# Two heads per key and query turn in the causal attention of a two-block transformer kernel, its first turn one round earlier, and three orders changed at seams

## The chip, the cores and the metric

The kernel runs on one core of one Trainium2 chip. The metric is the device time of one execution in microseconds (us); of the kernel before, three runs were timed, with a median of 1488.41 us (1486.58 to 1489.02). A core has TensorE (PE: matrix products and transposes into PSUM), VectorE (DVE), ScalarE (ACT), GpSimd (POOL) and SyncE (SP, which here only starts DMA transfers). Each engine works through its own list of instructions in order; semaphores tie them together.

## The reference, cut to what matters

Two blocks follow one another on x of 1024 tokens by 1024 channels: the first has grouped attention and a neighbourhood attention, the second a gated delta rule beside a dilated attention. All is float32. The change touches mainly the dilated attention of the second block:

```python
q, k, v = jnp.split(qkv, 3, axis=-1)                       # 8 heads of 64 channels
q = rms_norm(split_heads(q, ATT_HEADS), q_norm_w) * (ATT_HEAD_DIM ** -0.5)
k = rms_norm(split_heads(k, ATT_HEADS), k_norm_w)
for window, dilation in ((128, 1), (512, 4), (2048, 16)):
    o_p, lse_p = dilated_pattern(q, k, v, rel_bias, window, dilation)   # causal
o = sum(softmax(stack(lses)) * stack(outs))
```

The kernel computes the three patterns as one causal softmax over all keys, with a table that holds the bias and how many patterns a distance is in ("causal" below). Besides it, three small places are touched: the norm and projection at the start (`proj = rmsnorm(x) @ w_in`), the neighbourhood attention of block one ("near"), and the last rounds of the delta rule.

## The kernel before

**Products in float32.** Each product of float32 data is made from halves. A matrix is cast to a shortened form (`_hi`) by ACT, and DVE or POOL subtracts that from the original to get the rest (`_lo`). So every operand that is prepared costs a cast, then a subtraction that waits for it.

**Start (L405 to L450).** A token tile t of x is squared by ACT (L185), normalised by DVE (L194 to L201), turned by PE (L124, two halves of four 128x128 transposes), cast by ACT (L134) and subtracted by DVE (L140). PE then multiplies it by chunk 0 of the weights (L368). Chunk 1 of the weights comes through its own cast on ACT (L318, step t=3) and a subtraction on DVE (L334, `split_lo` at t=3). All later chunks are subtracted by POOL (`gpsimd`, L334).

**Near (L1195 to L1290).** Heads and row blocks are units u, two at a time. Every sixth unit ACT casts and DVE subtracts one 128-row piece kt of `w_out` (`ws.split_hi`, `ws.split_lo`), kt = u//6, from a transfer that SP started.

**Delta.** A chain of 16 chunks; the chunks of a round are inverted by a Newton-like iteration (L2158 and L2173 on PE, ACT copy L2452, DVE L2327 and L2330), whose result X is applied (L2184, L2196), and the state is stepped (L2215, L2230, L2239 on PE; L2349, L2358, L2369 on DVE). The order of every engine is written by hand with generators: `next(following)` lets the causal part put in its own steps between delta's, at eight places of the last two rounds, called round i=8 and round i=9 below.

**Causal (L2643 to L2960).** Eight heads with eight query blocks each make 64 units, ordered (7, 0, 6, 1, 5, 2, 4, 3) within a head. For a unit PE makes scores (L2785, L2786: query halves against one operand that holds the high key half on partitions 0 to 63 and the low one on 64 to 127), DVE adds the bias table and finds the maximum (L2865), ACT takes the exponential (L2927), PE transposes the probabilities (L2796), ACT or DVE copies them out (L2937, L2875), PE multiplies by v (L2810), and DVE divides (L2884). Before a head's scores, its keys and queries are turned in four parts ("preps": 512 tokens of k, 512 of k, 512 of q, 512 of q). For each part POOL writes the head's 64 channels twice side by side (`c_twice`, L2743), PE does four 128x128 transposes (L2773), ACT casts (L2922), DVE subtracts ("low", L2850 and L2852). Head h+1 is prepared in units 0, 1, 3 and 4 of head h, in PSUM bank 3. Head 0 is prepared in round i=9 of delta, each part in a PSUM bank of its own. After each unit's own work every engine does the unit's prep step, and none of it may be overtaken by what follows on the same engine.

```python
    PREP_AT = (0, 1, 3, 4)
    def prep_bank(h, part):
        return part + 1 if h == 0 else PREP_BANK
```

## Time and profile before

| | us |
|---|---|
| median of three timed runs | 1488.41 (1486.58 to 1489.02) |
| the profiled execution | 1485.48 |
| its span, as the profile has it | 1483.6 |
| PE busy | 1438.0 (97%) |
| DVE busy | 801.7 (54%) |
| ACT busy | 619.0 (42%) |
| POOL busy | 425.0 (29%) |

The clock granted to TensorE was full in all 40 slices of the profile (mean 0.997). A busy share says how much of the span an engine was at work; it does not say where PE, which is busy nearly all the time, still waits. That is read from the idle time that stands in brackets behind a row, with the instruction that ended it ("[1.37 <-DVE hT_lo L140]": 1.37 us idle, released by DVE's write of hT_lo at line 140). In a group of rows, "x8" means eight instructions in one stretch. The start of the span is time zero.

### The profile page before, as it was taken

Reading aid. Unit: us, or ns where it says so; the run is one execution under the profiler, and the core shown is the slowest. Engines: PE = TensorE matmul, PEld = TensorE weight load, DVE = VectorE, ACT = ScalarE, POOL = GpSimd, SP = SyncE. Lnnn points to the kernel's source line nnn. Section 1 sums busy time; section 2 is a strip of 40 time slices with the busy share of each in tenths; the row PEclk is TensorE's granted clock in tenths of the full one; section 3 lists DMA queues with packets and bytes.
Section 4 is the critical chain, followed back from the end, with each engine's and each line's share of the span. In section 5 each row is a group of like instructions: output and inputs, shape, how many; then the busy total and the mean of one; then the engine's idle time right before and its main releaser. Section 6 shows DMA issues by size and latency. Waiting matters only on the chain.

```text
span 1483.6 us, 30802 instructions
## 1 busy us (share of the span) xinstructions
PE 1438.0 (97%) x12682; PEld 1267.8 (85%) x12682; DVE 801.7 (54%) x1474; ACT 619.0 (42%) x1249; POOL 425.0 (29%) x527
## 2 busy tenths in 40 slices
PE   6999999989999999999999999999998998999998
PEld 6999998867777778878899999888897886888887
DVE  5238410149999878735420723452424776888431
ACT  5322121027777677632432113332325554777210
POOL 0212132110000277623202212221205884434320
PEclk9999999999999999999999999999999999999999
DMA  8313222000000043256325244433121021222342
GB/s 261 55 51 104 87 92 70 27 1 1 1 1 1 17 130 105 66 177 171 92 43 59 50 94 85 59 59 56 29 68 41 28 90 44 61 76 71 100 131 82
DMA packets 88017, 105.32 MB, mean 71 GB/s; under 512 B 25343, under 2 KB 72095, under 8 KB 87880
## 3 DMA queue, kind: packets, MB, share of 16 engines
q1 hardware_dynamic: 87880, 103.36, 27.0%
q8 instruction: 102, 1.67, 0.5%
q14 instruction: 35, 0.29, 0.1%
HBM read 80.20 MB, written 23.12 MB: 70 GB/s over the span
## 4 chain that ended last, share of the span: by engine, by line
PE 56%; DVE 4%; ACT 2%; DMA 1%; issue 1%; SPq 0%; POOL 0%; DVEq 0%; ACTq 0%
PE ps L368 22%; PE ps L1336 12%; PE ps L2810 2%; PE ps L1144 2%; PE ps L1128 2%; PE ps L2796 2%; PE ps L2785 1%; PE ps L2215 1%; PE ps L2158 1%; PE ps L2173 1%; DMA p_w_raw<-w_in 1%; PE ps L2773 1%; PE ps L1123 1%; PE ps L1122 1%; PE ps L2786 1%
## 5 line engine op out<-in xcount | busy, mean ns | idle before, releaser
L334 POOL TENSOR_TENSOR p_w_lo<-p_w_raw,p_w_hi 128x2048 fp32r<-128x2048 f32 (+1 forms) x27 | 127.3, 4716 | 506.9 <-ACT p_w_hi L318 506.9
L368 PE MATMUL ps<-p_w_hi,w_out_hi 128*128 128x256 f32 (+1 forms) x640 | 181.9, 284 | 0.4 <-ACT p_spill L393 0.3
L368 PE MATMUL ps<-p_w_hi,w_out_lo 128*128 128x256 f32 (+1 forms) x640 | 179.7, 281 | 0.0
L368 PE MATMUL ps<-p_w_lo,w_out_hi 128*128 128x256 f32 (+1 forms) x640 | 179.6, 281 | 0.0
L368 PE MATMUL ps<-p_w_hi,hT_hi 128*128 128x256 f32 x576 | 163.7, 284 | 1.9 <-DVE hT_lo L140 1.9
L368 PE MATMUL ps<-p_w_hi,hT_lo 128*128 128x256 f32 x576 | 162.7, 282 | 0.0
L368 PE MATMUL ps<-p_w_lo,hT_hi 128*128 128x256 f32 x576 | 162.6, 282 | 0.0
L368 PEld LDWEIGHTS ps<-p_w_hi,w_out_hi 128*128 128x128 f32 x640 | 120.5, 188 | 1.5 <-ACT p_spill L393 0.8
L368 PEld LDWEIGHTS ps<-p_w_lo,w_out_hi 128*128 128x128 f32 x640 | 120.8, 189 | 0.0
L368 PEld LDWEIGHTS ps<-p_w_hi,w_out_lo 128*128 128x128 f32 x640 | 120.6, 188 | 0.0
L368 PEld LDWEIGHTS ps<-p_w_hi,hT_hi 128*128 128x128 f32 x576 | 109.0, 189 | 2.3 <-DVE hT_lo L140 2.3
L318 ACT CAST p_w_hi<-p_w_raw 128x2048 fp32r<-128x2048 f32 (+1 forms) x28 | 53.5, 1909 | 137.0 <-DMA p_w_raw<-w_in 100.6
L368 PEld LDWEIGHTS ps<-p_w_lo,hT_hi 128*128 128x128 f32 x576 | 109.0, 189 | 0.0
L368 PEld LDWEIGHTS ps<-p_w_hi,hT_lo 128*128 128x128 f32 x576 | 109.0, 189 | 0.0
L897 ACT ACTIVATE tok<-ps,a_stat 128x1024 f32<-128x1024 f32 x64 | 72.4, 1131 | 43.6 <-DVE a_stat L848 43.6
L853 DVE TENSOR_TENSOR a_pt_lo<-ps,a_pt_hi 128x512 fp32r<-128x512 f32 x128 | 82.3, 685 | 15.3 <-ACT a_pt_hi L905 15.2
L393 ACT ACTIVATE p_spill<-ps 128x256 f32<-128x256 f32 x96 | 34.9, 385 | 132.9 <-PE ps L368 116.9
L905 ACT CAST a_pt_hi<-ps 128x512 fp32r<-128x512 f32 x128 | 68.8, 590 | 46.1 <-PE ps L794 46.1
L848 DVE TENSOR_REDUCE a_stat<-ps 128x1 f32<-128x1024 f32 x64 | 77.8, 1216 | 0.3 <-PE ps L784 0.3
L368 PE MATMUL ps<-w_out_hi,p_w_hi 128*128 128x512 f32 x192 | 76.2, 397 | 0.0
L368 PE MATMUL ps<-w_out_hi,p_w_lo 128*128 128x512 f32 x192 | 75.7, 394 | 0.0
L368 PE MATMUL ps<-w_out_lo,p_w_hi 128*128 128x512 f32 x192 | 75.5, 393 | 0.0
(299 smaller groups left out, 3585.0 us busy)
## 6 DMA issues: line engine op xcount, KB each, us to landing
p_w_raw<-w_in SPq DMA_DIRECT2D x26, 1024.0 KB, 8.0
s_gate<-p_spill SPq DMA_DIRECT2D x48, 128.0 KB, 1.8
kbT<-x SPq DMA_DIRECT2D x8, 512.0 KB, 6.9
b_w_raw<-w_out SPq DMA_DIRECT2D x8, 512.0 KB, 6.2
qT<-s_gate SPq DMA_DIRECT2D x8, 512.0 KB, 6.9
qT<-x SPq DMA_DIRECT2D x8, 512.0 KB, 3.5
s_x<-qT SPq DMA_DIRECT2D x8, 512.0 KB, 3.1
c_table<-s_line SPq DMA_DIRECT2D x8, 512.0 KB, 3.6
```

Source lines behind the costliest of these rows:

```text
L318: self.nc.scalar.copy(self.w_hi[:, c % 2, :, 0:w], self.raw[:, :, 0:w]).then_inc(self.w_hi_ready, 1)
L334: ops.tensor_tensor(self.w_lo[:, c % 2, :, 0:w], self.raw[:, :, 0:w], self.w_hi[:, c % 2, :, 0:w].bitcast(F32), ALU.subtract).then_inc(sel ...
L368: last = self.nc.tensor.matmul(out, lhs, rhs, start=(kt == 0 and i == 0), stop=(kt == KT - 1 and i == 2))
L393: op = self.nc.scalar.activation(dst, src, ACT.Silu if ch.silu else ACT.Copy)
L848: nc.vector.tensor_reduce(stat[:, 0, u:u + 1], s, AX.X, ALU.max, negate=True).then_inc(max_ready, 1)
L853: nc.vector.tensor_tensor(part(pt_lo, grp, half, i), ps[:, 4 + half, :].rearrange("p (c q) -> p c q", c=4), part(pt_hi, grp, half, i).bitc ...
L897: nc.scalar.activation(prob(u), s, ACT.Exp, bias=stat[:, 0, u:u + 1], accum_out=stat[:, 1, u:u + 1]).then_inc(prob_ready, 1)
L905: nc.scalar.copy(part(pt_hi, grp, half, i), ps[:, 4 + half, :].rearrange("p (c q) -> p c q", c=4)).then_inc(pt_hi_ready, 1)
L1128: last = nc.tensor.transpose(ps[:, 4 + u % 2, j * P:(j + 1) * P], prob[:, u % 4, j * P:(j + 1) * P], g.ident[:, :])
L1144: last = nc.tensor.matmul(ps[i * HD:(i + 1) * HD, 6 + u % 2, 0:HD], prob_t[:, u % 2, j * P + i * HD:j * P + (i + 1) * HD], value_tile(p, i ...
L1336: last = self.nc.tensor.matmul(self.ps[:, 4 + n % 4, :], a, b[:, kt, cols], start=(kt == 0 and i == 0), stop=(kt == KT - 1 and i == 2))
L2796: last = nc.tensor.transpose(ps[:, 4 + n % 2, (j - first) * P:(j - first + 1) * P], prob[:, u % 3, j * P:(j + 1) * P], g.ident[:, :])
```

## The change

Five things change.

1. **Preps by pairs of heads.** PE transposes 128 channels straight from the token tile `tok`, which are two heads at once. A set of four parts (now two of q, then two of k) serves a pair, so 16 transposes stand where 32 stood. The pair is prepared at units 2, 5, 8 and 11 of the sixteen units of the pair in front. POOL's copies `c_twice` go. ACT and DVE do two operations per part, one per head, on 64 partitions each. The second copy of a query half, on the other 64 partitions, is made by DMA from SBUF to SBUF (`double` on SP, four per q part), and scores wait for it (`q_doubled`). A key's low half goes to the other partitions by DVE's own write. There are four slots for keys and queries instead of two (`c_odd` is new).
2. **Pair 0 is prepared in round i=8** of delta instead of head 0 in round i=9, all four parts in one PSUM bank (bank 1). The scores of unit 0 go to banks 3 and 4, and stand before the last L2239 (`attend`).
3. **Start.** PE's first product waits for one half of tile 0 instead of both. The subtraction of weight chunk 1 moves from DVE to POOL.
4. **Near.** The cast and subtraction of `w_out` piece kt move six units later.
5. **SP** starts a head's bias table before its weight piece, instead of after.

The diff, cut to its core:

```diff
     def first_tensor(self, pe):
         self.norm.turn(pe, 0)
-        pe.wait_ge(self.norm.lo_ready, 2)
+        pe.wait_ge(self.norm.lo_ready, 1)
         self.multiply(pe, 0, 0, lambda: self.norm.turn(pe, 1))
...
             if t < NT:
                 self.norm.normalise(dve, t)
             self.norm.split_lo(dve, t - 1)
-            if t == 3:
-                self.split_lo(dve, self.nc.vector, 1)
...
-        pr.gpsimd(pool, 2, KEYS_AT + 1)
+        pr.gpsimd(pool, 1, KEYS_AT + 1)
...
-            if u % 6 == 4 and u // 6 < KT:
-                ws.split_lo(dve, nc.vector, u // 6)
+            if u % 6 == 4 and 0 < u // 6 <= KT:
+                ws.split_lo(dve, nc.vector, u // 6 - 1)
...
-            if u % 6 == 2 and u // 6 < KT:
-                ws.split_hi(act, nc.scalar.copy, u // 6)
+            if u % 6 == 2 and 0 < u // 6 <= KT:
+                ws.split_hi(act, nc.scalar.copy, u // 6 - 1)
...
-    k.sb("d_room2", [P, 2, H4, P])
+    g.osq = k.sb("d_osq", [P, 2, H4, P])[:, 0, :, :]
...
-    PREP_AT = (0, 1, 3, 4)
+    PREP_AT = (2, 5, 8, 11)
...
+        pair, at = u // (2 * NT) + 1, u % (2 * NT)
+        return [(pair, PREP_AT.index(at))] if at in PREP_AT and 2 * pair < ATT_HEADS else []
...
-        return 2 * (u % 2)
-        return part + 1 if h == 0 else PREP_BANK
+        return 2 * (u % 2) if u else 3
+        return 1 if pair == 0 else PREP_BANK
...
-    def half_of(t, h, part):
-        return t[:, h % 2, (part % 2) * 512:(part % 2) * 512 + 512]
+    def half_of(t, h, part, side):
+
+        return t[h % 4][side * HD:(side + 1) * HD, (part % 2) * 512:(part % 2) * 512 + 512]
...
+        def double(pair, part):
+            sp.wait_ge(low_ready, 8 * pair + 2 * part + 2)
+            for side in range(2):
+                h = 2 * pair + side
+                for m in (q_hi, q_lo):
+                    sp.dma_start(half_of(m, h, part, 1 - side).bitcast(F32), half_of(m, h, part, side).bitcast(F32)).then_inc(q_doubled, 16)
...
+        double(0, 0)
+        double(0, 1)
         sp.wait_ge(delta.s["o_summed"], NT)
         load_table(1)
         ws.load(sp, 0)
         ws.load(sp, 1)
         for h in range(2, ATT_HEADS):
+            if h % 2 == 0:
+                double(h // 2, 0)
+                double(h // 2, 1)
+            load_table(h)
             ws.load(sp, h)
-            load_table(h)
...
+        def turn_prep(pair, part):
+
+            if pair + part >= 1:
+                pe.wait_ge(low_ready, 8 * pair + 2 * part)
+            c0 = (0 if part < 2 else 512) + pair * P
             for j in range(4):
-                src = twice[:, part % 2, j, :, :].rearrange("p a d -> p (a d)")
-                last = nc.tensor.transpose(ps[:, prep_bank(h, part), j * P:(j + 1) * P], src, g.ident[:, :])
+                last = nc.tensor.transpose(ps[:, prep_bank(pair, part), j * P:(j + 1) * P],
+                                           g.att_tok[:, 4 * (part % 2) + j, c0:c0 + P], g.ident[:, :])
             last.then_inc(prep_turned, 1)
...
-            pe.wait_ge(low_ready, 4 * h + 4)
+            pe.wait_ge(low_ready, 8 * (h // 2) + 8)
+            pe.wait_ge(q_doubled, 128 * (h // 2) + 128)
...
-        for _ in range(4):
+        pe.wait_ge(delta.s["khatT_ready"], NT)
+        pe.wait_ge(delta.s["u_copied"], NT - 1)
+        for part in range(4):
+            turn_prep(0, part)
             yield
+        yield
+        yield
         pe.wait_ge(delta.s["attnT_ready"], NT)
         pe.wait_ge(delta.s["A_ready"], NT)
         pe.wait_ge(delta.s["X0_ready"], NT)
-        pe.wait_ge(delta.s["u_copied"], NT)
-        for part in range(4):
-            turn_prep(0, part)
-            yield
         scores(0)
+        yield
+        yield
         scores(1)
...
+        def low(pair, part):
+
+            bank = prep_bank(pair, part)
+            for side in range(2):
+                dve.wait_ge(high_ready, 8 * pair + 2 * part + side + 1)
+                turned_side = ps[side * HD:(side + 1) * HD, bank, :]
+                h = 2 * pair + side
+                if part < 2:
+                    hi, dst = half_of(q_hi, h, part, side), half_of(q_lo, h, part, side)
+                else:
+                    hi, dst = half_of(kk, h, part, side), half_of(kk, h, part, 1 - side)
+                nc.vector.tensor_tensor(dst, turned_side, hi.bitcast(F32), ALU.subtract).then_inc(low_ready, 1)
...
+        def high(pair, part):
+
+            act.wait_ge(prep_turned, 4 * pair + part + 1)
+            if pair >= 2:
+                act.wait_ge(scores_ready, NT * (2 * pair - 2))
+            for side in range(2):
+                dst = half_of(q_hi if part < 2 else kk, 2 * pair + side, part, side)
+                nc.scalar.copy(dst, ps[side * HD:(side + 1) * HD, prep_bank(pair, part), :]).then_inc(high_ready, 1)
```

In round i=8 of delta, PE's list shows where the four parts stand (L2773 was the prep's transpose; it is L2763 now, and all of delta's lines are two lower: L2158 is L2156, L2173 is L2171). Before, from the Newton step that follows the last L2196 but one:

```order
L2158 MATMUL ps<-d_X,d_Al 64x64 x8
L2173 MATMUL ps<-d_Z,d_T 64x64 x8
L2215 MATMUL ps<-d_S,d_wq 128x128 x4
L2158 MATMUL ps<-d_X,d_Al 64x64 x8
L2230 MATMUL ps<-d_vnew,d_ktail 64x128 x8
L2173 MATMUL ps<-d_Z,d_T 64x64 x8
L2158 MATMUL ps<-d_X,d_Al 64x64 x8
L2215 MATMUL ps<-d_S,d_wq 128x128 x4
L2173 MATMUL ps<-d_Z,d_T 64x64 x8
L2158 MATMUL ps<-d_X,d_Al 64x64 x8
L2230 MATMUL ps<-d_vnew,d_ktail 64x128 x8
L2173 MATMUL ps<-d_Z,d_T 64x64 x8
```

Now, with `tok` as the source of the preps:

```order
L2156 MATMUL ps<-d_X,d_Al 64x64 x8
L2171 MATMUL ps<-d_Z,d_T 64x64 x8
L2213 MATMUL ps<-d_S,d_wq 128x128 x4
L2763 MATMUL ps<-ident,tok 128x128 x4
L2156 MATMUL ps<-d_X,d_Al 64x64 x8
L2228 MATMUL ps<-d_vnew,d_ktail 64x128 x8
L2763 MATMUL ps<-ident,tok 128x128 x4
L2171 MATMUL ps<-d_Z,d_T 64x64 x8
L2156 MATMUL ps<-d_X,d_Al 64x64 x8
L2213 MATMUL ps<-d_S,d_wq 128x128 x4
L2763 MATMUL ps<-ident,tok 128x128 x4
L2171 MATMUL ps<-d_Z,d_T 64x64 x8
L2156 MATMUL ps<-d_X,d_Al 64x64 x8
L2228 MATMUL ps<-d_vnew,d_ktail 64x128 x8
L2763 MATMUL ps<-ident,tok 128x128 x4
L2171 MATMUL ps<-d_Z,d_T 64x64 x8
```

Each part from the second on stands directly in front of an L2171 group, or of one that leads to it. On DVE, in the same round, the subtractions of the preps (`c_q_lo`, `c_kk`) have come between; before:

```order
L2349 TENSOR_TENSOR d_vnew<-d_u,ps 64x512
L2358 TENSOR_TENSOR d_S<-d_Sg,ps 128x512
L2327 TENSOR_TENSOR d_X<-d_X,ps 128x256
L2330 STREAM_TRANSPOSE d_T<-d_X 128x256
L2349 TENSOR_TENSOR d_vnew<-d_u,ps 64x512
L2327 TENSOR_TENSOR d_X<-d_X,ps 128x256
L2330 STREAM_TRANSPOSE d_T<-d_X 128x256
L2358 TENSOR_TENSOR d_S<-d_Sg,ps 128x512
L2327 TENSOR_TENSOR d_X<-d_X,ps 128x256
```

Now:

```order
L2347 TENSOR_TENSOR d_vnew<-d_u,ps 64x512
L2850 TENSOR_TENSOR c_q_lo<-ps,c_q_hi 64x512 x2
L2356 TENSOR_TENSOR d_S<-d_Sg,ps 128x512
L2850 TENSOR_TENSOR c_q_lo<-ps,c_q_hi 64x512 x2
L2325 TENSOR_TENSOR d_X<-d_X,ps 128x256
L2328 STREAM_TRANSPOSE d_T<-d_X 128x256
L2347 TENSOR_TENSOR d_vnew<-d_u,ps 64x512
L2850 TENSOR_TENSOR c_kk<-ps,c_kk 64x512 x2
L2325 TENSOR_TENSOR d_X<-d_X,ps 128x256
L2328 STREAM_TRANSPOSE d_T<-d_X 128x256
L2356 TENSOR_TENSOR d_S<-d_Sg,ps 128x512
L2850 TENSOR_TENSOR c_kk<-ps,c_kk 64x512 x2
```

Two subtractions stand in front of each `d_S` or `d_X` that follows them. In the causal part, DVE's list in the third head (head 2) of before has two preps within five units, one subtraction each:

```order
L2865 ISA c_stat 128x1
L2875 COPY c_prob_t<-ps 128x512
L2850 TENSOR_TENSOR c_kk<-ps,c_kk 64x512
L2881 RECIPROCAL c_stat<-c_stat 128x1
L2884 TENSOR_SCALAR tok<-ps,c_stat 128x64
L2865 ISA c_prob,c_stat<-ps,c_table 128x256
L2865 ISA c_stat 128x1
L2850 TENSOR_TENSOR c_kk<-ps,c_kk 64x512
L2881 RECIPROCAL c_stat<-c_stat 128x1
L2884 TENSOR_SCALAR tok<-ps,c_stat 128x64
L2865 ISA c_prob,c_stat<-ps,c_table 128x768
```

At the same place now, two subtractions stand together behind the sixth unit's bias (768 wide) and its copy:

```order
L2862 ISA c_prob,c_stat<-ps,c_table 128x256
L2862 ISA c_stat 128x1
L2878 RECIPROCAL c_stat<-c_stat 128x1
L2881 TENSOR_SCALAR tok<-ps,c_stat 128x64
L2862 ISA c_prob,c_stat<-ps,c_table 128x768
L2862 ISA c_stat 128x1
L2872 COPY c_prob_t<-ps 128x384
L2850 TENSOR_TENSOR c_q_lo<-ps,c_q_hi 64x512 x2
L2878 RECIPROCAL c_stat<-c_stat 128x1
L2881 TENSOR_SCALAR tok<-ps,c_stat 128x64
L2862 ISA c_prob,c_stat<-ps,c_table 128x384
```

The order of the units' own work has not moved.

## Rows read from the trace of the kernel before

**Rows 1.** The page, part 1: engine, busy us, share of the span, instructions.

```profile
PE 1438.0 (97%) x12682; PEld 1267.8 (85%) x12682; DVE 801.7 (54%) x1474; ACT 619.0 (42%) x1249; POOL 425.0 (29%) x527
```

**Rows 2.** Windows: length, busy PE, PEld, DVE, ACT, POOL; sixth and last head, second without preps.

```profile
1334.16:1350.15 15.99, 15.81 (x222) 13.98 (x221) 14.06 (x42) 11.74 (x27) 5.77 (x6) 1.00 0.23 69
1366.12:1380.02 13.90, 13.77 (x209) 12.01 (x209) 12.07 (x40) 9.91 (x23) 4.11 (x4) 1.00 0.26 76
```

**Rows 3.** Groups by form, the preps' transposes: count, busy, mean ns, idle before.

```profile
L2773 PE MATMUL ps<-ident,c_twice 128*128 128x128 f32 x128 | 19.6, 275 | 3.0 <-DVE c_kk L2850 1.4 <-DVE c_q_lo L2852 1.3 <-DVE d_vnew L2349 0.3
```

**Rows 4.** Timeline of DVE (start, length): the first bias of heads 0, 1, 2.

```profile
1253.32 1.22 DVE L2865 CUSTOM_DVE_ANT_0 c_prob<-ps,c_table 128x1024 f32<-128x1024 f32 x1 [0.20 <-issue]
...
1269.23 1.22 DVE L2865 CUSTOM_DVE_ANT_0 c_prob<-ps,c_table 128x1024 f32<-128x1024 f32 x1
...
1286.18 1.22 DVE L2865 CUSTOM_DVE_ANT_0 c_prob<-ps,c_table 128x1024 f32<-128x1024 f32 x1 [0.16 <-PE ps L2786]
```

**Rows 5.** Timeline of ACT in head 0: the two table loads.

```profile
1264.71 1.28 ACT L3070 ACT_TABLE_LOAD   x1
...
1267.22 1.28 ACT L2927 ACT_TABLE_LOAD   x1
```

**Rows 6.** Waits of PE: engine and line waited for, total, times, longest.

```profile
PE ps L124 <- DVE hT_lo L140: 1.6, 2, 1.4
PE ps L2773 <- DVE c_kk L2850: 1.4, 2, 1.1
```

**Rows 7.** Timeline of the last rounds of delta, all engines.

```profile
1235.47 0.41 DVE L2327 TENSOR_TENSOR d_X<-d_X,ps 128x256 f32<-128x256 f32 x1
...
1238.52 0.42 DVE L2327 TENSOR_TENSOR d_X<-d_X,ps 128x256 f32<-128x256 f32 x1
...
1241.24 0.41 DVE L2327 TENSOR_TENSOR d_X<-d_X,ps 128x256 f32<-128x256 f32 x1
...
1241.71 1.09 PE L2184 MATMUL ps<-d_vb,d_X 64*64 64x128 f32 x16
...
1245.89 0.58 ACT L2922 CAST c_kk<-ps 128x512 fp32r<-128x512 f32 x1
...
1246.51 0.69 DVE L2850 TENSOR_TENSOR c_kk<-ps,c_kk 64x512 fp32r<-64x512 f32 x1 [0.54 <-ACT c_kk L2922]
...
1249.93 0.66 PE L2773 MATMUL ps<-ident,c_twice 128*128 128x128 f32 x4 [0.35 <-DVE d_vnew L2349]
...
1250.63 0.59 ACT L2922 CAST c_q_hi<-ps 128x512 fp32r<-128x512 f32 x1 [0.38 <-PE ps L2773]
```

**Rows 8.** Timeline of the start, ACT, DVE and PE.

```profile
20.07 1.91 ACT L318 CAST p_w_hi<-p_w_raw 128x2048 fp32r<-128x2048 f32 x1
...
22.02 2.29 DVE L334 TENSOR_TENSOR p_w_lo<-p_w_raw,p_w_hi 128x2048 fp32r<-128x2048 f32 x1
...
22.16 1.05 ACT L185 ACTIVATE qbT<-kbT 128x1024 f32<-128x1024 f32 x1
...
24.84 1.28 DVE L201 SCALAR_TENSOR_TENSOR qbT<-kbT,n_stat,qbT 128x1024 f32<-128x1024 f32 x1
...
26.04 1.28 DVE L140 TENSOR_TENSOR hT_lo<-ps,hT_hi 128x512 fp32r<-128x512 f32 x2
...
26.87 1.16 PE L124 MATMUL ps<-ident,qbT 128*128 128x128 f32 x8 [1.37 <-DVE hT_lo L140]
```

**Rows 9.** Timeline of DVE, the same three products at two places.

```profile
944.43 3.93 DVE L1912 SCALAR_TENSOR_TENSOR conv_y<-conv_in,p_conv_w,conv_y 128x1024 f32<-128x1024 f32 x3
...
994.13 8.18 DVE L1912 SCALAR_TENSOR_TENSOR conv_y<-conv_in,p_conv_w,conv_y 128x1024 f32<-128x1024 f32 x3
```

**Rows 10.** Timeline of POOL at the second of these places.

```profile
995.19 4.72 POOL L334 TENSOR_TENSOR p_w_lo<-p_w_raw,p_w_hi 128x2048 fp32r<-128x2048 f32 x1 [14.61 <-ACT p_w_hi L318]
```

**Rows 11.** Timeline of near, ACT and PE.

```profile
529.18 1.05 ACT L1287 CAST w_out_hi<-b_w_raw 128x1024 fp32r<-128x1024 f32 x1 [1.25 <-DMA b_w_raw<-w_out]
...
530.77 1.15 PE L1144 MATMUL ps<-b_v,b_prob_t 128*64 128x64 f32 x32 [0.95 <-ACT b_prob_t L1241]
```

More of the change, by code:

```diff
@@ L2653, in causal_part @@
     n_units = len(units)
-    PREP_AT = (0, 1, 3, 4)
+    PREP_AT = (2, 5, 8, 11)
     PREP_BANK = 3
-    v, table, kk, q_hi, q_lo = g.c_v, g.c_table, g.c_kk, g.c_q_hi, g.c_q_lo
-    prob, prob_t, twice = g.c_prob, g.c_prob_t, g.c_twice
+    v, table = g.c_v, g.c_table
+    kk, q_hi, q_lo = ([both[:, 0, :], both[:, 1, :], g.c_odd[:, n, 0, :], g.c_odd[:, n, 1, :]]
+                      for n, both in enumerate((g.c_kk, g.c_q_hi, g.c_q_lo)))
+    prob, prob_t = g.c_prob, g.c_prob_t
     ws = WeightSplit(nc, k, "c_w_", g.w_out2, w_hi, w_lo, g.c_raw, delta.weights)
@@ L2819, in tensor @@
         pe.wait_ge(delta.s["X0_ready"], NT)
-        pe.wait_ge(delta.s["u_copied"], NT)
-        for part in range(4):
-            turn_prep(0, part)
-            yield
         scores(0)
+        yield
+        yield
         scores(1)
@@ L2831, in tensor @@
             turn_probs(u)
-            for h, part in preps(u):
-                turn_prep(h, part)
+            for pair, part in preps(u):
+                turn_prep(pair, part)
             if u >= 2 and u % 2 == 0:
@@ L2885, in store @@
                                     None, ALU.mult).then_inc(out_stored, 1)
-        for _ in range(4):
-            yield
         for part in range(4):
             low(0, part)
+            yield
+        for _ in range(4):
             yield
@@ L2908, in vector @@
             empty(u)
-            for h, part in preps(u):
-                low(h, part)
+            for pair, part in preps(u):
+                low(pair, part)
         for u in range(n_units - 3, n_units):
@@ L2938, in empty @@
                                    ps[:, 4 + n % 2, 0:(end - first) * P]).then_inc(pt_by["act"], 1)
-        for _ in range(4):
-            yield
         for part in range(4):
             high(0, part)
+            yield
+        for _ in range(4):
             yield
@@ L2950, in scalar @@
             empty(u)
-            for h, part in preps(u):
-                high(h, part)
+            for pair, part in preps(u):
+                high(pair, part)
             if u + 2 < n_units:
```

53 lines of the change are left out of this document (6 added, 47 removed).

## The prediction

> **What bounds the kernel now.** I read the busy times first. PE is busy 1438.0 of 1483.6 us [rows 1], so the other engines count only where PE waits for them, and what is taken from PE counts only where nothing else comes last at once. The views after that were the windows by head, the groups by form, the waits of PE, and the timelines of the four places that the change touches. In the causal part a head takes, by the first window, 15.99 us with PE busy 15.81, DVE 14.06 and ACT 11.74 [rows 2]: PE sets the pace, and DVE has 1.93 us to spare. The last head, which prepares no follower, takes 13.90, by the second [rows 2]. So one set of 16 transposes is worth 15.99 - 13.90 = 2.09 us, or 131 ns each. The delta rounds are another regime: there PE waits at each step of a chain through PE, ACT and DVE. At the start PE waits for the low halves of the token tiles, 1.6 us in two waits [rows 6].
>
> **Causal part.** Before, seven heads (0 to 6) carry a set of 16 transposes for their follower. Now three pairs (0 to 2) carry one set each. Four sets go: 4 x 2.09 = 8.36 us, the most that can be had here. The reader should not multiply 64 removed transposes by their mean of 275 ns [rows 3]: that is 17.6 us, but the durations overlap, and the head's own windows say 131 ns. The Trainium skill, page "TensorE: Matmul & The Clock Gate", Part 4: PE-mode transpose, gives about 275 ns for one in a kernel's context. By that figure the four sets in the causal part would be worth 64 x 0.275 = 17.6 us; the row has the same 275 as a duration, and the windows show that it is no spacing.
>
> DVE decides what arrives of the 8.36. Its eight subtractions per pair and 14.06 us per head stay, while PE's period would fall to 15.99 - 1.05 = 14.94 per head, so DVE is at 94%. The two subtractions of a part stand together, 2 x 0.69 [rows 7], where a single 0.69 stood. The spare of DVE is (14.94 - 14.06) / 8 = 0.11 us per unit, so behind unit 5 about 0.5 of the second 0.69 reaches the bias of unit 8 and PE. I take 0.5 per pair, an estimate from these rows. Pairs 1 and 2 gain 2.09 - 0.5 = 1.59 each. Pair 0 has two table loads of 1.28 on ACT in front of a cast on which DVE waits in order [rows 5]; its two heads took 32.86 [rows 4] against 2 x 15.99 = 31.98 already. I put 0.24 more on it: 1.35. Head 6 had a set and has none now: 2.09. Sum: 2 x 1.59 + 1.35 + 2.09 = 6.6. Bounds: 8.36 if DVE's pairs of operations hide, 2.09 if DVE sets the period and only head 6 gains.
>
> The doubling DMAs are four of 64 x 512 floats per q part, 0.52 MB. The DMA moves 69 GB/s there at a share of 0.23 [rows 2], so some 300 GB/s in full: an estimate of 1.7 us per part, and 7.6 at the mean rate. The scores of the next pair come ten units (some 20 us) after the second q part, for pair 0 some 15 us. I cost them at nothing; with the cover gone it would be the 1.7 at pair 0. POOL's copies were off PE's path, and no gain. The table in front of the weights on SP is for a head later: nothing.
>
> **Seam.** Pair 0's four parts now stand in round i=8, where d_X follows at 1235.47, 1238.52 and 1241.24 and the apply at 1241.71 [rows 7]. All four share a PSUM bank. So a part costs, as a chain: from its transposes to the cast 1250.63 - 1249.93 = 0.70, from the cast to the subtraction 1246.51 - 1245.89 = 0.62, and two subtractions of about 0.67 with their spacing: 2.65 us. In that time the next part's transposes wait on PE, with delta's L2171 (L2173 before) behind them, and DVE stands at the subtraction with delta's d_X and d_S behind it. I laid delta's steps out around this. The first d_X has two parts in front of it, of which one overlaps other waits: 1235.47 becomes 1238.1. Part 2 lies between it and the next, and takes 5.0 instead of 3.05: 1238.52 becomes 1243.1. Part 3 comes before the third, 4.4 instead of 2.72: 1241.24 becomes 1247.5. The apply starts at about 1248.0 instead of 1241.71: +6.3. Round i=9 is freed of its four parts. Its own chain (S times wq, v_new, S) ran at its pace with them; only behind the last v_new they stood on it, at 1249.93 where PE did transposes before L2239. That and the scores in front of it give back 0.7. The first bias moves from 1253.32 [rows 4] to 1258.9: **+5.6**. Bounds: -0.7 (all four parts vanish in PE's waits of round 8) and +6.3 (nothing is given back). I take 5.6, since both queues are in order and the bank admits one part at a time. Before, each had its own bank and no part waited for a part.
>
> **Start.** DVE's subtraction of chunk 1 takes 2.29 at 22.02, in front of tile 4's chain: L201 at 24.84, hT_lo at 26.04, and PE's turn at 26.87 after 1.37 idle [rows 8], 2.03 behind the start of L201. Taken away, that chain starts when ACT's square L185 is done, 22.16 + 1.05 and a read-out, at 23.4. Two small operations between took 0.53 (from 24.31, the subtraction's end, to 24.84); L201 would begin at 23.95, and PE at 26.0: -0.9. Waiting for one low half of tile 0 lets PE begin up to 0.6 earlier, but chunk 1's transfer and cast, which come next, do not move; I cost that at nothing (at best -0.5, so -1.4 in all, the idle time). But POOL's subtraction starts when the cast ends, at 22.0, and takes 4.72 [rows 10], until 26.7; L201 has two inputs in SBUF and falls into it. Three such DVE products took 3.93 at 944.43, and 8.18 at 994.13 [rows 9], where the same POOL line ran from 995.19 to 999.91 [rows 10]: 4.25 longer, nearly the whole of POOL's 4.72. So DVE stands while POOL runs. L201 works from 26.7 on, the turn comes at 26.7 + 2.03 = 28.75, and the start loses 28.75 - 26.87 = **+1.9**. Bounds: -1.4, and +3.3 (L201 lengthened by the whole 4.25: -0.9 + 4.25).
>
> The Trainium skill, page "SBUF — State Buffer", section "Who interferes with whom", says that a DVE instruction with two SBUF inputs contends with a GpSimd instruction that reads SBUF, and that the shared read port is locked for a whole instruction. It speaks against this part of the change. With the rule the start is +1.9, without it -0.9; the 8.18 beside 3.93 agree with the rule.
>
> **Near.** The first cast of w_out on ACT waits 1.25 for its DMA, and PE's L1144 then waits 0.95 for ACT's copy behind it [rows 11]. Six units later the data lies there. Gain 0.95; bounds 0 (another copy comes late) and 1.2. The last piece is still split well before w_out is used.
>
> **Sum.** -6.6 + 5.6 + 1.9 - 0.95 = -0.05. The profiled execution took 1485.48, 1.9 more than its span; the median is 1488.41, 2.93 above it. I keep that distance: 1485.5 - 0.05 + 2.93 = **1488.4**, no change.
>
> **Rivals.**
> B: the delta round hides its preps. For it: before, PE and DVE both waited at most steps there, and PE has room for 16 transposes. Against: one bank, and two subtractions in front of each d_X. The seam then gives -0.7 instead of +5.6: -6.6 - 0.7 + 1.9 - 0.95 = -6.35, thus 1482.1.
> D: POOL's subtraction does not hold up L201, because the two meet otherwise than at 994.13. Start -0.9: the sum is -2.85, thus 1485.6. For it: there is one such meeting among my rows. Against: its size.
> C, the slower side: DVE sets the period of pairs 0 to 2. Its in-order list takes two subtractions that wait for two casts, eight times in the sum, and ACT's casts come in pairs between exponentials. Then only head 6 gains: -2.09 + 5.6 + 1.9 - 0.95 = +4.5, thus 1492.9. It decides once DVE's waits per head exceed 14.94 - 14.06 = 0.9 us. For it: PE already waits for these subtractions, 1.4 us [rows 6] and 1.3 [rows 3]. Against: in before's windows DVE is 1.93 us idle per head without holding PE.
>
> **Chances.** Forecast 0.48, B 0.15, D 0.20, C 0.17. About 0.2% (3.0 us) is what a measurement of this kernel can tell from no change. Faster by more: B whole, D half, and 0.06 of the forecast's spread: 0.31. Slower by more: C for 0.15 and 0.04 of the forecast: 0.19. The same: 0.50. The range leaves out the far halves of B and of C, some 0.16: 1482.5 to 1492.5. The forecast's own range is 1485.5 to 1490.5: the causal part may give 1.8 more, the seam 0.7 cost more or 1.0 less, the start 1.4 more.
>
> **What would show it.** Right: the first bias of head 0 some 5 to 6 us later relative to round 8's beginning, with PE's L2763 waiting for `c_q_lo` and `c_kk`; windows of a pair at 30.2 to 30.6 instead of 31.98; the last two heads at 13.9 each; L201 of tile 4 lasting over 3 us or starting late beside POOL's L334 at 22; PE's wait at L1144 gone. Wrong: a seam of the old length (B), a turn of tile 4 before 26.2 (D), pairs that take 31.5 or more with DVE busy in every gap (C). A new wait of PE for `q_doubled` would overturn the cost of nothing that I gave the DMAs.

## The result, and the profile after

Over eleven runs each, the changed kernel took 1495.96 us (1491.20 to 1498.60) and the kernel before 1487.62 (1486.12 to 1489.02): ratio 1.0053, 95% interval 1.0042 to 1.0064. I had forecast 1488.4 and no change, with a range up to 1492.5. The forecast was wrong: the kernel is 0.5% slower, and outside the range. One execution of one variant below (the filler's) ran at a mean granted clock of 0.556 and took 2346.02 us; its ratio leaves it out.

The page after, its first part and the row of the granted clock in 40 slices (tenths of full speed):

```profile
span 1496.5 us, 30632 instructions
...
PE 1444.5 (97%) x12618; PEld 1271.3 (85%) x12618; DVE 807.7 (54%) x1473; ACT 622.3 (42%) x1249; POOL 407.5 (27%) x496
...
PEclk9999999999999999999999999999998997999999
```

PE has 64 instructions fewer than in [rows 1], and yet is busy 6.5 us longer. The clock row points to the reason: before it had no slice under 9, now one shows 8 and one 7. The 7 is the seam. The 8 lies near 1130 us, where both kernels fall to the lower clock: the 9s before do not mean a full clock everywhere, as 6.8 us there were at the lower level already, and 10.2 in this profile. The profiled run's mean clock was 0.988, against 0.997 before.

Points of the two timelines, each the start of the same instruction, show where the 12.9 us of the profiled runs came from (1496.5 - 1483.6; this profiled run is one of the slower of its eleven). A step is by how much the distance between the two kernels grew since the point above:

| point | before | after | step |
|---|---|---|---|
| tile 4's turn (PE L124) | 26.87 | 28.68 | +1.81 |
| tile 5's turn | 33.57 | 36.88 | +1.50 |
| L1144 (now L1142) before w_out's first cast | 526.24 | 529.70 | +0.15 |
| the next L1144 [rows 11] | 530.77 | 533.20 | -1.03 |
| d_X in front of delta's last round 8 steps | 1231.92 | 1235.88 | +1.53 |
| first bias of head 0 [rows 4] | 1253.32 | 1267.99 | +10.71 |
| first bias of head 2 | 1286.18 | 1301.11 | +0.26 |
| first bias of head 4 | 1318.17 | 1333.01 | -0.09 |
| first bias of head 6 | 1350.15 | 1364.88 | -0.11 |
| first bias of head 7 | 1366.12 | 1378.75 | -2.10 |
| end | 1483.6 | 1496.5 | +0.27 |

The start, timeline of DVE, POOL and PE after (start, length, instruction, idle before and its releaser), to be laid beside [rows 8]:

```profile
22.28 4.57 POOL L334 TENSOR_TENSOR p_w_lo<-p_w_raw,p_w_hi 128x2048 fp32r<-128x2048 f32 x1 [21.84 <-ACT p_w_hi L318]
...
24.17 3.76 DVE L201 SCALAR_TENSOR_TENSOR qbT<-kbT,n_stat,qbT 128x1024 f32<-128x1024 f32 x1
...
28.68 1.16 PE L124 MATMUL ps<-ident,qbT 128*128 128x128 f32 x8 [3.03 <-DVE hT_lo L140]
```

L201 takes 3.76 us instead of 1.28 and ends about 1.1 us behind POOL's L334: it stood. The seam (the last rounds of delta and the first scores), timeline of DVE and PE after, to be laid beside [rows 7]:

```profile
1242.38 0.42 DVE L2325 TENSOR_TENSOR d_X<-d_X,ps 128x256 f32<-128x256 f32 x1
...
1242.90 1.12 PE L2156 MATMUL ps<-d_X,d_Al 64*64 64x64 f32 x16 [2.00 <-issue]
1243.95 2.07 PE L2213 MATMUL ps<-d_S,d_wq 128*128 128x128 f32 x8
...
1248.97 0.42 DVE L2325 TENSOR_TENSOR d_X<-d_X,ps 128x256 f32<-128x256 f32 x1
...
1255.45 0.42 DVE L2325 TENSOR_TENSOR d_X<-d_X,ps 128x256 f32<-128x256 f32 x1
```

From 1235.88 the three d_X are 6.50, 13.09 and 19.57 us away; before, from 1231.92, they were 3.55, 6.60 and 9.32. And PE's own work is slow: eight matmuls of L2213 take 2.07 where they took 1.16. Windows after (length, busy PE, PEld, DVE, ACT, POOL, then the granted clock, the DMA share, GB/s): from the d_X at 1235.88 to the first bias, ten-microsecond stretches within it, a pair of heads, and the seventh head:

```profile
1235.88:1267.99 32.11, 24.27 (x278) 20.26 (x278) 15.73 (x27) 9.16 (x17) 3.15 (x4) 0.73 0.15 34
1240.00:1250.00 10.00, 6.44 (x74) 5.55 (x74) 5.48 (x10) 3.27 (x6) 1.04 (x1) 0.59 0.48 105
1250.00:1260.00 10.00, 8.42 (x120) 7.08 (x116) 4.23 (x7) 3.17 (x6) 2.08 (x2) 0.72 0.01 2
...
1301.11:1333.01 31.90, 30.62 (x426) 26.38 (x425) 28.07 (x85) 24.33 (x53) 6.83 (x4) 1.00 0.35 100
1364.88:1378.75 13.87, 13.87 (x206) 12.25 (x205) 11.41 (x38) 9.96 (x23) 3.79 (x3) 1.00 0.44 135
```

The clock was at its lower level (1.2 of 2.4 GHz) for 13.7 us from about 1242, that is from the middle of PE's 2.00 us of idle in front of 1242.90. A pair of heads takes 31.90 us, two heads of before 31.98 [rows 2]: nearly nothing of the removed transposes arrived. The seventh head takes 13.87.

The runs also tell what the clock is worth. Over 17 runs of the changed kernel the time falls with the run's mean granted clock by 0.92 us per 0.001; over 115 of the kernel before, by 0.98. The means of the clock are 0.9912 and 0.9957, so by my estimate 0.0045 x 0.95 per 0.001 = 4.3 us of the difference is clock. Where both kernels had 0.995, they took 1491.3 (three runs) and 1489.5 (26 runs).

### The profile page after: what moved, and what is told of

The parts are those of the page before. It is cut to its first block, busy times and chain, and to the rows that moved or that the text cites. A ratio compares the mean times of both kernels' runs of the same rounds, so it can differ in the third digit from the quotient of the medians.

```text
span 1496.5 us, 30632 instructions
## 1 busy us (share of the span) xinstructions
PE 1444.5 (97%) x12618; PEld 1271.3 (85%) x12618; DVE 807.7 (54%) x1473; ACT 622.3 (42%) x1249; POOL 407.5 (27%) x496
## 4 chain that ended last, share of the span: by engine, by line
PE 55%; DVE 4%; ACT 2%; issue 2%; DMA 1%; POOL 0%; DVEq 0%; SPq 0%; ACTq 0%
PE ps L368 22%; PE ps L1334 12%; PE ps L1142 2%; PE ps L1126 2%; PE ps L2802 2%; PE ps L2788 2%; PE ps L2213 1%; PE ps L2156 1%; PE ps L2777 1%; PE ps L2171 1%; DMA p_w_raw<-w_in 1%; PE ps L1119 1%; PE ps L1121 1%; PE ps L1120 1%; PE ps L2778 1%
## 5 line engine op out<-in xcount | busy, mean ns | idle before, releaser
L334 POOL TENSOR_TENSOR p_w_lo<-p_w_raw,p_w_hi 128x2048 fp32r<-128x2048 f32 (+1 forms) x28 | 130.2, 4650 | 508.0 <-ACT p_w_hi L318 508.0
```

What stands on the lines that cost most here:

```text
L334: ops.tensor_tensor(self.w_lo[:, c % 2, :, 0:w], self.raw[:, :, 0:w], self.w_hi[:, c % 2, :, 0:w].bitcast(F32), ALU.subtract).then_inc(sel ...
```

## The experiments

The runs come from several chips, each with its own runs of the kernel before beside it. "Under the changed kernel" is therefore taken from the ratios to before (1.0053 for the changed kernel), times 1488 us.

**Start.** First, chunk 1's subtraction back on DVE in the changed kernel.

```diff
             self.norm.split_lo(dve, t - 1)
+            if t == 3:
+                self.split_lo(dve, self.nc.vector, 1)
...
-        pr.gpsimd(pool, 1, KEYS_AT + 1)
+        pr.gpsimd(pool, 2, KEYS_AT + 1)
```

> The changed kernel with the subtraction of weight chunk 1 back on DVE (at t=3); PE's first product still waits for one low half only. Theory (POOL's subtraction holds up DVE's L201 of tile 4, 3.76 us instead of 1.28, and PE's 3.03 us of idle there is followed by a stretch at half clock that moves tile 5's turn from +1.8 to +3.3): L201 lasts 1.3 again, tile 4 is turned at about 26.9, the clock does not fall before 45 us, tile 5 is turned at 33.6 instead of 36.9, and the whole is 3.3 us faster than the changed kernel: 1492.5 by the median. Rival (the loss belongs to the earlier first product, or to the clock alone, whose fall comes anyway): tile 5 stays at 36 or later, the gain is under 1 us. A second rival: only the queueing of 1.8 us goes and the half clock stays.

Median 1494.52 (ratio to before 1.0036, 1.0024 to 1.0047). L201 lasted 1.28, tile 4 was turned at 26.98 and tile 5 at 33.67, and the clock did not fall there. The profile shows the whole 3.2 us at tile 5; of the time only 1.4 us came by the medians and 2.5 by the ratios. What held back the rest is not shown; the clock in the seam was as low as in the changed kernel. Then the reverse: the POOL part alone, put into the kernel before.

> The kernel before, with the subtraction of weight chunk 1 on POOL instead of DVE, and nothing else. Theory (DVE's L201 with two inputs in SBUF stands while POOL's subtraction runs): L201 of tile 4 lasts 3.5 us or more, tile 4 is turned at 28.5 to 28.9 instead of 26.87, and the time is 1.8 us higher, 3.3 if the clock also falls behind PE's idle time of 3 us. Rival (the loss of the changed kernel's start needs the earlier first product too): under 0.5 us.

Median 1490.87 (1.0016, 1.0007 to 1.0024): +2.2 us, between the 1.8 and the 3.3 that I had expected. Tile 4 was turned at 28.98, tile 5 at 37.25, and L201 reads

```profile
24.46 3.77 DVE L201 SCALAR_TENSOR_TENSOR qbT<-kbT,n_stat,qbT 128x1024 f32<-128x1024 f32 x1
```

The rival (it needs the earlier first product) is out. In all eleven profiles with the subtraction on POOL, L201 took 3.75 to 3.78 us, in the eight others 1.28 or 1.29. The 8.27 us between the tiles' turns instead of 6.70 are a stretch at the lower clock: the windows from tile 4's turn to tile 5's, of the changed kernel and then of the first experiment, hold the same 56 matmuls:

```profile
28.68:36.88 8.20, 8.20 (x56) 8.08 (x57) 3.15 (x6) 1.62 (x4) 0.00 (x0) 0.79 1.17 279
```

```profile
26.98:33.67 6.69, 6.69 (x56) 6.57 (x57) 3.15 (x6) 1.70 (x5) 0.00 (x0) 1.00 1.12 289
```

**Near**, alone in the kernel before (the two conditions of the diff).

> The kernel before, with the cast and subtraction of w_out pieces in near six units later, and nothing else of the change. Theory (the 0.95 us that PE waits at L1144 for ACT's copy, behind a cast that waits for its DMA, goes): that wait is gone and the time is 0.9 us lower, which five rounds may not tell from nothing (0.9994). Rival (the wait moves to another piece): no difference and a new wait on PE at L1144 of about 1 us.

Median 1486.99 (0.9990, 0.9981 to 0.9999): -1.7 us, its interval from -2.8 to -0.1. Where [rows 11] had 0.95 us idle, L1144 has none, and PE waited for `b_prob_t` 0.2 us in all.

**Seam and clock.** Ten transposes of the identity, whose result nothing reads, behind each of two L2171 groups (the "filler"):

```diff
+    FILL = 10
...
                 last.then_inc(s["dX_ready"], 1)
+                if t == N - 1 and l in (3, 4):
+                    for n in range(FILL):
+                        nc.tensor.transpose(ps[:, 3, 256 + 128 * (n % 2):384 + 128 * (n % 2)], g.ident[:, :], g.ident[:, :])
```

> The changed kernel with ten additional transposes of the identity into an unused half of a PSUM bank behind the third and the fourth L2171 group of delta's last inversion, where PE was idle for 2.0 and 1.6 us; they compute nothing that is read. Theory (5 of the seam's 10.7 us are the clock at half from about 1242 to 1256, which fell after PE's idle stretches): the granted clock stays at 1.0 through this stretch, the step of the first bias is 5 to 6 us behind before's instead of 10.7, the run-to-run scatter shrinks, and the median falls by 3 to 5 us, to about 1492. Rival (the clock's record is a consequence and the chain alone makes the length, or the waits have other places): the added transposes take their 1.3 us each in part from the chain, and the kernel is 0 to 2 us slower. If the clock falls elsewhere instead, the total stays.

Median 1494.09 (1.0033, 1.0022 to 1.0045), 3.0 us under the changed kernel. Windows of this run, from the same d_X to the first bias, and the stretch in which the changed kernel had 0.59:

```profile
1235.27:1262.36 27.09, 20.23 (x298) 16.98 (x298) 15.71 (x26) 9.06 (x17) 3.15 (x4) 1.00 0.18 41
1240.00:1250.00 10.00, 8.44 (x135) 7.31 (x132) 5.92 (x11) 3.91 (x9) 1.30 (x2) 1.00 0.49 107
```

More work on PE, and the stretch is 5.0 us shorter, because the clock stayed up. So the seam's 10.7 us are two things: 27.09 - 21.40 = 5.7 us of chain (the filler's own time may be in it), and 5.0 us of clock. It is one profile with the filler; but all eight profiles with the parts where the changed kernel has them, and no filler, show a fall in this stretch, of 6.8 to 13.7 us. Next, the four parts at every second place (ACT's casts likewise).

```diff
         for part in range(4):
+            if part == 2:
+                pe.wait_ge(delta.s["u_copied"], NT)
             turn_prep(0, part)
             yield
...
+            yield
...
         for part in range(4):
+            yield
             low(0, part)
             yield
```

> The changed kernel with pair 0's four parts at every second place between delta's steps (two in round 8, two in round 9) and DVE's subtractions one place behind the transposes and casts; still one PSUM bank. Theory (a part's chain of transposes, casts and two subtractions stood in series with delta's steps, 2.65 us per part, because the bank and the in-order lists admit no overlap): with a place between them the chain runs beside delta's, the first bias comes 4 to 8 us earlier than in the changed kernel, and the clock falls less; the median is 4 to 8 us lower. Rival (the work of eight subtractions and eight casts itself fills the rounds): under 2 us. A cost could be that the last subtractions now stand right before the scores: at most 1.5 us.

Median 1491.10 (1.0014, 1.0005 to 1.0023), 5.8 us under the changed kernel. From the d_X at 1235.15 to the first bias it took 26.43 with one short fall of the clock (3.4 us). The last d_X of round 8 was still 14.10 behind instead of 9.32: two parts cost 4.8 us there. Then all four parts back in round 9, with four banks:

> The changed kernel with pair 0's four parts in round i=9 of delta, as head 0's were before, each in a PSUM bank of its own (1 to 4), the scores of unit 0 in banks 0 and 1 behind them; casts and subtractions two per part. Theory (the series of bank, casts and subtractions in front of delta's steps costs the seam 5.7 us, and the clock that falls behind its idle time another 5): delta's round 8 runs as before, the clock does not fall in it, and the first bias comes 2 to 4 us later than before's relative to the last d_X of the round (eight casts and subtractions instead of four, and the doubled queries land 2.4 us after the second part's), so the kernel is 6 to 9 us faster than the changed kernel, at 1488 to 1490. Rival (the round doesn't matter, the doubled count of casts and subtractions does): the seam stays over 8 us behind before's.

Median 1491.95 (1.0024, 1.0015 to 1.0033), 4.3 us under the changed kernel and 2 over what I expected. Round 8 ran as before (d_X 3.55, 6.60 and 9.32 behind), but the first bias came 5.4 us later than before's behind it, where I had expected 2 to 4, since the first scores waited, timelines of DVE and PE:

```profile
1253.31 2.85 DVE L2847 TENSOR_TENSOR c_kk<-ps,c_kk 64x512 fp32r<-64x512 f32 x4 [0.40 <-ACT c_kk L2917]
...
1258.87 0.77 PE L2777 MATMUL ps<-c_kk,c_q_hi 128*128 128x512 f32 x1 [4.24 <-DMA c_q_lo<-c_q_lo]
```

Here is the wait for the doubled queries that I had priced at nothing: in the changed kernel round 8 buys its cover. Not all of the 4.24 us is theirs: the scores also need the last key subtraction, which ended at 1256.16 (1253.31 + 2.85), so the transfers alone held PE for 2.7 us. SP issued the eight from 1250.25 to 1256.38, mostly 0.6 us apart, and in the median they land 2.4 us after their issue.

**Pace of a pair.** DVE's subtractions a unit later, then also ACT's casts behind the exponentials:

```diff
-            for pair, part in preps(u):
+            for pair, part in preps(u - 1) if u else []:
                 low(pair, part)
```

> The changed kernel with DVE's two subtractions of a prep part done one unit later (behind unit u+1's own work), casts and transposes where they are. Theory (in the causal part DVE stands at the subtraction for ACT's two casts, and PE then waits for DVE, so pairs take 31.9 us instead of the 30.3 that I had forecast): the waits of DVE for c_odd and c_q_hi go, a pair takes 30.0 to 30.6, and pairs 0 to 2 give 1.3 to 1.9 each, 4 to 5.5 us in all. Rival (ACT's two casts in front of the exponentials are what is late, DVE's place doesn't matter): pairs stay at 31.5 or more and the total within 1 us. Rival (DVE's busy time itself is the period): as before, but with DVE without idle.

> The changed kernel with DVE's subtractions one unit later (as in the run with lows later) and ACT's two casts of a part behind the exponentials of unit u+2 instead of in front of them. With the subtractions alone moved a pair took 31.4 us instead of 31.9. Theory (what is left is ACT's 1.19 us of casts in front of an exponential that PE waits for two units later): pairs take 30.2 to 30.8, and the kernel gains 2 to 3.5 us over the one with lows later alone. Rival (DVE's 14.1 us of work per head with its waits for PE's scores is the period now): pairs stay at 31.2 to 31.5. A third way: the casts, now late, make the subtractions late, and pairs take over 31.9.

Medians 1494.66 (1.0036) and 1491.69 (1.0022); a pair took 31.4 us in both, so moving the casts did nothing for it, and the two medians differ as their clocks do (0.989 and 0.992). The 0.5 us compare with 2.0 that were missing per pair. Then the two sides apart, one per unit:

> The changed kernel with the two casts and the two subtractions of a part no longer side by side: ACT casts the first head's half in unit u and the second's in u+1, DVE subtracts in u+1 and u+2. With both subtractions one unit later and together, a pair took 31.4 us, and DVE's 1.40 us pair of subtractions stood in front of a unit of small width. Theory (it is the burst of 1.4 us in DVE's in-order list that PE waits for, not DVE's total work): pairs take 30.0 to 30.7, 1.2 to 1.9 us less than in the changed kernel each, and the kernel is 4 to 6 us faster than the changed one. Rival (DVE's 14 us per head and its waits are the period): 31.2 to 31.5 again.

Median 1493.73 (1.0036). A miss: 31.80 per pair. The last subtraction now comes in unit 13, and PE waits 1.2 us per pair for it at the next scores (L2777 for `c_kk` or `c_odd`). Then other places, `PREP_AT = (0, 3, 8, 11)`:

> The changed kernel with the q parts of pairs 1 to 3 at units 0 and 3 of the pair in front instead of 2 and 5 (PREP_AT 0, 3, 8, 11). In the changed kernel a head with parts at 2 and 5 took 16.86 us, one with parts at 8 and 11 (0 and 3 of its own eight) 15.03, where one without parts takes 13.88: 1.5 us per part against 0.58. Theory (it is the place within the head: behind units 2 and 5 DVE's list has no slack for two casts and two subtractions, behind 0 and 3 it has): both heads of a pair take about 15.0, a pair 30.1, and the kernel is 4 to 5.5 us faster than the changed one. Rival (q parts are dear wherever they stand, by the doubling transfers and the waits behind them): the first head stays at 16.5 to 17.

Median 1496.51 (1.0045) at a mean clock of 0.990 in the middle run. The pair took 31.23, both heads 15.6: 0.7 us less, where I had expected 1.8. Then less work for DVE at these places:

```diff
-        return "dve" if piece == 1 or u % 4 == 3 else "act"
+        return "dve" if piece == 1 else "act"
```

> The changed kernel with q parts at units 0 and 3 as in the run before it, and one kind of work taken off DVE: the copies of the turned probabilities of every fourth unit (0.4 and 0.7 us, two per head) go to ACT, which is busy 24.2 of a pair's 31.2 us. Theory (DVE's in-order list is full: in 31.2 us it is busy 28.2, and its timeline shows hardly a gap over 0.15 us, the rest goes between instructions; so DVE's amount of work is the period once the bursts are placed well): a pair takes 29.9 to 30.6. Rival (the period is a chain of waits between units that doesn't depend on DVE's amount): it stays at 31.2, or rises as ACT's copies come later.

Median 1494.41 (1.0044). Windows of a pair, first without and then with the copies moved:

```profile
1300.82:1332.05 31.23, 30.39 (x426) 26.48 (x425) 28.16 (x85) 24.24 (x53) 6.84 (x4) 1.00 0.38 103
```

```profile
1295.21:1326.42 31.21, 30.33 (x426) 26.49 (x425) 26.32 (x80) 26.04 (x57) 6.83 (x4) 1.00 0.37 103
```

DVE has 1.84 us less to do, and the pair takes 31.21. My theory (DVE's amount) fell. The timeline of the run with (0, 3, 8, 11) shows a wait instead, which comes once in each head, on ACT, DVE and PE around unit 3:

```profile
1311.35 1.18 ACT L2920 CAST c_q_hi<-ps 64x512 fp32r<-64x512 f32 x2 [0.62 <-PE ps L2763]
...
1311.96 1.41 DVE L2850 TENSOR_TENSOR c_q_lo<-ps,c_q_hi 64x512 fp32r<-64x512 f32 x2 [0.36 <-ACT c_q_hi L2920]
1313.40 0.16 DVE L2878 RECIPROCAL c_stat<-c_stat 128x1 f32<-128x1 f32 x1
1313.60 0.28 DVE L2881 TENSOR_SCALAR tok<-ps,c_stat 128x64 f32<-128x64 f32 x1
...
1314.03 0.45 PE L2802 MATMUL ps<-c_v,c_prob_t 128*64 128x64 f32 x8 [0.42 <-DVE tok L2881]
```

PE multiplies by v in even units only, two units at once, and there needs a store (L2881) that stands in DVE's list behind the subtractions of the odd unit in front. An even unit's part has a whole unit of PE's time before that.

In the changed kernel itself, with parts at 2, 5, 8 and 11, this wait stands only once in the pair, behind unit 11. Its timeline of PE has two more, for copies of turned probabilities:

```profile
1312.42 0.44 PE L2788 MATMUL ps<-ident,c_prob 128*128 128x128 f32 x2 [0.36 <-DVE c_prob_t L2872]
...
1318.20 0.57 PE L2802 MATMUL ps<-c_v,c_prob_t 128*64 128x64 f32 x12 [0.38 <-ACT c_prob_t L2935]
...
1330.60 0.45 PE L2802 MATMUL ps<-c_v,c_prob_t 128*64 128x64 f32 x8 [0.43 <-DVE tok L2881]
```

The first is DVE's copy of unit 3, which stands in its list behind the subtractions of unit 2; the second is ACT's copy behind the casts of unit 5 and an exponential. Places 0 and 3 removed these two (31.90 to 31.23), and brought a second wait for the store.

**Versions put together.** The first: chunk 1's subtraction on DVE, sides apart, pair 0's parts at four spread places; then the same with the unread transposes.

> A version put together: the changed kernel with chunk 1's subtraction on DVE, the sides apart in the causal part, and pair 0's parts at the first, third, fifth and sixth place of delta's last two rounds (banks 1, 1, 3, 4; subtractions one place later; scores of unit 0 in banks 0 and 1 at the last place). By the theories that stand: start -0.2 against before, near -0.95, seam +2 to +4 (half the series of the changed kernel), pairs 0 to 2 together -3 to -4.8, last pair -2.1: 4 to 5 us faster than before if the clock doesn't fall in the seam, so 1484 to 1486; if it does for 7 to 14 us, 1487 to 1489, no different from before. Rival (pairs stay at 31.4): 1487 without the fall.

> The version put together, with the ten unread transposes in each of two idle stretches of round 8. Theory (idle stretches there are what lets the clock fall): higher mean clock and less scatter than without them, and 0 to 3 us faster, about 1485. Rival (with the parts spread the idle stretches are short enough, as before's are, where the clock held): the filler costs its own time in the chain, up to 1.3 us each, 1 to 2 us slower.

1490.03 (1.0018, 1.0010 to 1.0027) and 1490.45 (1.0017, 1.0008 to 1.0025): both misses, slower than before. The pairs took 31.8, the scores of unit 0 waited 2.6 us for the last k part, and the clock fell there or just behind, filler or not; in round 8, where it fell for 3.4 us in the first of the two, it held with the filler. The second version prepares heads 0 and 1 as before, pairs 1 to 3 by pairs:

> A second version put together. Heads 0 and 1 are prepared as in the kernel before (single heads, doubled by POOL, head 0 in round i=9 with four banks, head 1 in units 0, 1, 3 and 4), pairs 1 to 3 by pairs (pair 1 at units 6, 8, 11 and 12, the others at 0, 3, 8 and 11); chunk 1's subtraction on DVE; near as changed. Theory (the seam's loss is the place and the series of pair 0's parts, and the pace is the places): the seam and the clock as before (21.4 us from the second last step to the first bias, no fall of the clock), heads 0 and 1 together 32.5 to 33.5, pairs at 30.1, last heads 13.9 each: 6 to 7 us faster than before, 1481 to 1483. If only the place in the head fails, 2 to 3 us faster. Rival (the gain of fewer transposes can't be had because DVE is the bound): no faster than before by over 2 us.

1484.48 (0.9974, 0.9963 to 0.9985), 3.8 us faster than before, where I had expected 6 to 7. The seam took 21.39 (1232.65 to 1254.04) and the clock held in it, but pairs 1 and 2 took 31.05 and 31.22 instead of 30.1, and heads 0 and 1 together 34.94 instead of 32.5 to 33.5 (before: 32.86). With the copies on ACT:

> The second version put together, with the same copies moved to ACT. Theory: pairs 1 and 2 at 29.9 to 30.6 instead of 31.2, 1.2 to 2.6 us faster than the version without, heads 0 and 1 up to 1 us faster too, where DVE has six or more subtractions; about 1482.5. Rival: ACT, with the table loads in head 0 and the casts, becomes late, and the version is slower than the one without by up to 2 us.

1485.12 (0.9975, 0.9965 to 0.9985): no difference, a miss. Last, all parts of the pairs at even units:

```diff
-    PREP_AT = (0, 3, 8, 11)
-    PAIR1_AT = (6, 8, 11, 12)
+    PREP_AT = (0, 4, 8, 12)
+    PAIR1_AT = (6, 8, 10, 12)
```

> The second version put together (copies as before, not moved to ACT), with all parts of pairs 1 to 3 at even units: 6, 8, 10 and 12 for pair 1, 0, 4, 8 and 12 for the others. PE multiplies by v only in even units, and needs there the store (L2881) that stands in DVE's list directly behind the subtractions of an odd unit's part; once per head PE waits 0.4 us at that place, however much work DVE has. Theory (that store, late behind two casts and two subtractions of an odd unit, is what is left of the pace): the wait of L2802's successor line for the store goes, pairs 1 and 2 take 30.0 to 30.6 instead of 31.2, and the version gains 1 to 2.4 us. Rival (some other chain between units): 31.2 again.

1483.42 (0.9966, 0.9954 to 0.9978): 4.5 us faster than before by the medians, 5.1 by the ratio, and 12.9 under the changed kernel: the best of all. A pair:

```profile
1304.59:1334.70 30.11, 30.11 (x426) 26.31 (x424) 27.94 (x86) 24.07 (x53) 6.86 (x4) 1.00 0.39 107
```

No wait of PE is left in it; its amount of work is the same as at 31.23 (426 matmuls). But an even unit is not enough. Pair 1, now with a part at unit 10, in front of a unit that DVE copies, again has the wait for that copy:

```profile
1285.05 0.44 PE L2826 MATMUL ps<-ident,c_prob 128*128 128x128 f32 x2 [0.60 <-DVE c_prob_t L2920]
```

Heads 0 and 1 took 36.00 us in this version, 3.1 more than before's 32.86 (with a fall of the clock of 3.4 us in them): the best version still loses there part of what it gains. The changed kernel again, beside the others:

> The changed kernel once more, word for word, beside the others on one chip. All theories: about 8 us slower than before in the median, by the runs' own clocks spread along a line of about 1 us per 0.001 of mean granted clock; at the same clock as before's, 2 to 3 us slower. If the time did not go with the clock in this larger set, the part that I give the clock would fall.

1495.54 (1.0048, 1.0032 to 1.0063), as expected.

## Why the prediction was wrong, step by step

- **Start, +1.9: right, +1.81.** I had the turn at 28.75, it came at 28.68. POOL's hold on DVE is shown in both directions (experiments on the start). The 1.5 us of clock that followed are in the item on the clock below.
- **Near, -0.95: right, -1.03**, and the wait is gone.
- **Seam, +5.6: right as a chain, 5.7** at full clock (the run with filler). I had the first d_X of the three 2.6 us later relative to the stretch's beginning, and the last 6.3; with the filler they were 2.95 and 6.8 later. That the sum fits to 0.1 is in part luck: round 9 gave back 1.1 where I had 0.7.
- **Causal, -6.6: the first step that failed.** Between the first bias of head 0 and of head 7 stand 110.76 us instead of 112.80: -2.0, or -2.8 in the run whose clock held (110.00). The term was "I take 0.5 per pair"; measured is 2.0 for pairs 1 and 2, so that only head 6 gave its 2.1. Pair 0 gave 0.5 with the clock held, where I had 1.35. That is rival C in its outcome, but not in its mechanism: it is not DVE's rate, since 1.84 us less of work moved nothing (shown with the parts at 0, 3, 8 and 11). It is the place of the parts: two casts and two subtractions delay what stands behind them in the same list, in the changed kernel DVE's copy behind unit 2, ACT's copy behind unit 5 and DVE's store behind unit 11, and PE waits for each. I had followed the second subtraction to the bias of unit 8 only. With the parts at 0, 4, 8 and 12 the pair took 30.11, 1.87 us under before's, more than the 1.59 I had forecast.
- **The clock: the second step that failed, by absence.** The prediction took TensorE's clock as full everywhere. It fell for 3.4 us at the start and for 13.7 us and twice 3.4 us around the seam. In the profiled run it cost 1.5 and 5.0 us in these places; over the runs my estimate is 4.3 us in the mean. That alone puts the forecast's 1488.4 at 1492.7, and with the 3.8 us that the causal part did not give at full clock (6.6 - 2.8), at 1496.5, against 1495.96.
- **The doubling transfers: priced rightly at nothing here**, since round 8 gives them their time. With that cover gone I had 1.7 us; put in round 9 they held PE for 2.7.
- **Rival B** (the round hides the preps) is out: two parts in round 8 cost 4.8 us even when spread. **Rival D** (POOL does not hold up L201) is out.

The +1.53 us in front of the delta rounds is mostly scatter between executions. No edit touches the lists of PE, ACT or DVE between near's last product and that d_X, and the stretch took 596.4 (before) to 598.6 us over all nineteen profiles, 597.9 in that of the changed kernel. It holds the fall of the clock near 1130 us: the seven profiles in which that lasted 10.2 us took 597.8 in the mean, the twelve with 6.8 took 597.2, so the longer fall goes with some 0.6 us. What decides its length stays open.

## What to carry to other kernels

Where PE is busy nearly always, an added idle stretch can cost twice: its own length, and the clock behind it. Look for the longest wait of PE that a change adds, and price it both ways. Work that is prepared ahead belongs behind units after which nothing in the same in-order list is due; follow every instruction that stands behind it (here a copy, another copy and a store), and who waits for each, not only the largest. And before an engine's amount of work is called the bound, take some of it away: a busy share of 90% with no gap in the timeline looked like one and was none.

## What the runs showed of the hardware

- The time of one execution goes with its mean granted clock, in these two kernels, by 0.92 to 0.98 us per 0.001 of clock. The spread between runs of the changed kernel, 7.4 us, is nearly all that (correlation -0.98 over 17 runs).
- The clock behind PE's idle stretch at the start: of eleven profiles with about 3 us of idle there (2.98 to 3.50), nine show the fall (tile 5 comes 8.0 to 8.3 us behind tile 4) and two don't (6.7; the filler's and the one with the sides apart). Of eight with 1.37 to 1.84 us, one shows it (the second version with copies on ACT, 26.95 to 35.16), and it is the one with 1.84. So in these profiles idle time does not decide the fall alone, but it goes with how often it comes.
- Ten transposes that nothing reads, in each of two stretches of idle, made the seam around them 5.0 us shorter (one profile).
- L201 on DVE, with two inputs in SBUF, took 3.76 and 3.77 us when it met POOL's L334, and 1.28 without POOL beside it. The Trainium skill, page "SBUF — State Buffer", section "Who interferes with whom", says that a DVE instruction with two SBUF inputs contends with a GpSimd one that reads SBUF; these traces agree.
- A DVE subtraction from PSUM of 64 partitions takes as long as one of 128 (0.69 us for 512 columns), and an ACT cast too (0.59): a part split by heads costs either engine twice what the same data in one instruction does.
